# Experts in the order of their token counts, with places of 256 down to 32 tokens, in a mixture-of-experts kernel

## The reference

```python
def _moe(h, l, w_router, b_router, w_e_gate, w_e_up, w_e_down, w_s_gate, w_s_up, w_s_down):
    t = h.reshape(-1, shp[-1])                          # 576 tokens in all, 1024 wide
    s = jax.nn.sigmoid((t @ w_router[l]).astype(jnp.float32))
    _, sel = lax.top_k(s + b_router[l].astype(jnp.float32), TOP_K)        # TOP_K = 8 of 64
    g = jnp.take_along_axis(s, sel, axis=-1)
    g = g / jnp.sum(g, axis=-1, keepdims=True) * ROUTED_SCALE
    gates = ...                                         # g at the chosen experts, 0 elsewhere
    out = (jax.nn.silu(t @ w_s_gate[l]) * (t @ w_s_up[l])) @ w_s_down[l]
    for es in groups_of_8_experts:                      # w_e_gate, w_e_up: 1024 x 128, w_e_down: 128 x 1024
        a = jnp.einsum('nd,edf->nef', t, w_e_gate[l, es])
        u = jnp.einsum('nd,edf->nef', t, w_e_up[l, es])
        hid = jax.nn.silu(a) * u * gates[:, es, None]
        out = out + jnp.einsum('nef,efd->nd', hid, w_e_down[l, es])
    return out.reshape(shp)
```

## Time and profile before

| | us |
|---|---|
| median of 3 runs | 1312.42 (1308.63 to 1316.77) |
| the profiled execution | 1310.58 |
| its span, first to last instruction | 1308.6 |
| PE busy in the span | 1184.5 |
| gate_up's products (L1815) and down's (L1836) | 308.7 and 161.6 |
| turn_x (L1799) | 88.7 |
| granted clock, mean over the span | 0.962 of full |

### The profile page before, as it was taken

One profiled execution on the slowest core, in us unless ns is written; L12 is line 12 of the kernel. 1 busy time (PEld: TensorE's weight loads), 2 busy tenths in 40 slices (PEclk: granted clock), 3 DMA queues, 4 the chain that ended last, 5 costly groups with the idle time before them and its releaser, 6 DMA issues.

```text
span 1308.6 us, 26951 instructions
## 1 busy us (share of the span) xinstructions
PE 1184.5 (91%) x10827; PEld 719.5 (55%) x10827; DVE 552.3 (42%) x1349; ACT 390.0 (30%) x953; POOL 384.7 (29%) x447
## 2 busy tenths in 40 slices
PE   4899998899989898899769999999999999999796
PEld 1698885766744555454435555555555555555342
DVE  5418880243255477245627532332332222222245
ACT  3333331333345477111312222222222222222211
POOL 2233333423310232001012443434433434434200
PEclk8799998999989899899979999999999999999999
DMA  9222226543270000301629978878778778787296
GB/s 368 86 81 83 84 83 213 186 169 117 75 274 1 1 1 1 154 33 57 253 79 367 390 277 315 308 275 334 289 282 322 284 296 320 274 330 234 70 418 227
DMA packets 61738, 262.05 MB, mean 200 GB/s; under 512 B 24190, under 2 KB 24270, under 8 KB 47662
## 3 DMA queue, kind: packets, MB, share of 16 engines
q1 hardware_dynamic: 27648, 180.68, 37.1%
q0 software_dynamic: 33968, 79.66, 16.9%
HBM read 297.81 MB, written 53.69 MB: 269 GB/s over the span
## 4 chain that ended last, share of the span: by engine, by line
PE 66%; DMA 17%; DVE 8%; issue 5%; ACT 3%; POOL 2%; SPq 0%; POOLq 0%; DVEq 0%; ACTq 0%
PE bank L1815 15%; PE bank L1836 9%; DMA x_got<-x_dram,idx_tok 8%; PE bank L1670 5%; PE bank L1383 4%; PE bank L1799 4%; PE bank L1385 4%; PE bank L1384 4%; DMA pairs<-pair_dram 4%; PE bank L1489 3%; DMA pair_dram<-out_rows,idx_pair 2%; PE bank L1565 2%; PE bank L1411 1%; PE bank L1609 1%; PE bank L1821 1%
## 5 line engine op out<-in xcount | busy, mean ns | idle before, releaser
L1815 PE MATMUL bank<-slot,xt 128*32 128x256 f32 x5376 | 308.7, 382 | 12.3 <-issue 8.8
L1815 PEld LDWEIGHTS bank<-slot,xt 128*32 128x32 f32 x5376 | 180.2, 111 | 162.8 <-issue 68.3
L1836 PE MATMUL bank<-slot,hid_t 128*32 128x512 f32 x1344 | 161.6, 598 | 0.7 <-ACT hid_t L1348 0.7
L1048 POOL DMA_INDIRECT pair_dram<-out_rows,idx_pair x84 | 86.2, 1026 | 231.0 <-DVE out_rows L2304 182.7
L1383 PE MATMUL bank<-h_hi,w_hi 128*128 128x288 f32 x480 | 146.3, 305 | 0.0
L1384 PE MATMUL bank<-h_lo,w_hi 128*128 128x288 f32 x480 | 142.7, 297 | 0.0
L1385 PE MATMUL bank<-h_hi,w_lo 128*128 128x288 f32 x480 | 142.5, 297 | 0.0
L2304 DVE COPY out_rows<-bank 128x512 f32<-128x512 f32 x84 | 58.1, 692 | 171.0 <-DMA pair_dram<-out_rows,idx_pair 101.0
L656 POOL TENSOR_TENSOR w_lo<-w_stage,w_hi 128x1024 fp32r<-128x1024 f32 x29 | 69.6, 2402 | 131.2 <-ACT w_hi L1097 131.1
L1031 POOL DMA_INDIRECT x_got<-x_dram,idx_tok x84 | 85.8, 1021 | 72.4 <-DVE idx_tok L2282 43.2
L1354 ACT COPY out_rows<-bank 128x512 f32<-128x512 f32 x84 | 49.3, 587 | 168.5 <-DMA pair_dram<-out_rows,idx_pair 114.5
(11 more groups left out here) (338 smaller groups left out, 1565.9 us busy)
## 6 DMA issues: line engine op xcount, KB each, us to landing
slot<-in_w_moe SPq DMA_DIRECT2D x65, 1536.0 KB, 9.5
w_stage<-in_w_ada SPq DMA_DIRECT2D x32, 512.0 KB, 4.7
pairs<-pair_dram SPq DMA_DIRECT2D x16, 1024.0 KB, 9.9
w_stage<-in_w_in SPq DMA_DIRECT2D x30, 512.0 KB, 3.6
resid<-in_w_ada SPq DMA_DIRECT2D x2, 2048.0 KB, 13.2
w_out_sb<-in_w_out SPq DMA_DIRECT2D x1, 4096.0 KB, 15.2
o_t<-in_x_t SPq DMA_DIRECT2D x4, 576.0 KB, 5.6
feat<-in_w_ada SPq DMA_DIRECT2D x1, 2048.0 KB, 18.4
```

The costliest lines, as they stand in the source:

```text
L1048: g.indirect_dma_start(pair_dram, bass.IndirectOffsetOnAxis(ap=idx_pair[:, j, c:c + 1], axis=0), out_rows[:, i % 2, :], None, bounds_check ...
L1815: ins = mm(bank[2 + i % 2][r, 0:2 * P], xt[:, i % 2, k, r], slot_of(load)[:, 2 * P * k:2 * P * (k + 1)], start=(k == 0), stop=(k == KD - 1 ...
L1836: ins = mm(bank[4 + 2 * (i % 2) + c][r, :], hid_t[:, i % 2, r], slot_of(load)[:, 2 * D + 512 * c:2 * D + 512 * c + 512], start=True, stop= ...
```

## The change

The experts are sorted by their token counts at run time, and each place has a size by rank. The 64 ranks in groups of eight have 8, 4, 3, 3, 2, 2, 1 and 1 units of now 32 tokens (`CAPACITY`), 256 tokens down to 32. There are again 48 further places, of 64 tokens (two units), for what goes beyond an expert's own place. That is 192 + 96 = 288 units and 72 steps of four. With the counts above, 7 of the 48 further places are in use (22 before), and further place o is the o-th that is needed.

The places stand in eight like blocks of nine steps. Block g holds one rank of each group (8k + g) and six further places (8k + g):

| step of the block | places, with their units |
|---|---|
| 0, 1 | group 0 (8) |
| 2 | group 7 (1), further 0 (2), group 1 (first of 4) |
| 3 | group 1 (3 more), further 1 (first of 2) |
| 4 | further 1 (second), group 6 (1), group 2 (first two of 3) |
| 5 | group 2 (third), further 2 (2), group 3 (first of 3) |
| 6 | group 3 (2 more), further 3 (2) |
| 7 | group 4 (2), further 4 (2) |
| 8 | group 5 (2), further 5 (2) |

The six slots are parted: the shared expert and the ranked places go round slots 0 to 3 in their order, loaded by SP; the further places go round slots 4 and 5, loaded by POOL. A ranked place's address is now known only at run time: SP reads a row number from `idx_w` into a register ahead of each load, after the wait for the slot. Loads of ranked places start once `idx_w` is there.

The lists are made by unit in place of by expert: PE multiplies a choice matrix with the experts' values for three tiles of 128, 128 and 32 units (`unit_products`), ACT and DVE copy them and drop what belongs to an earlier unit (`find_units`), and DVE sorts four rounds (`PART // 8`) per tile: the first tile ahead of the loop, the second in steps 1 to 4, the third in steps 5 to 8, one round in a step. PE turns the second and third tile's lists at steps 6 and 11. Counting, ranking and the row numbers are worked out ahead of the loop, with PE's shared products cut into pieces between them. The gates' arithmetic leaves `choose` and goes into steps 12 to 16 as `find_gates`. POOL fills 52 small tables in place of 11 before it waits for the output projection.

The core of the diff:

```diff
-UNIT, PART = 96, 32
-N_OVER = (N_PROMPT + N_SAMPLE) * TOP_K // (UNIT + 1) + 1
+PART = 32
+CAPACITY = (8, 4, 3, 3, 2, 2, 1, 1)
+BEYOND, N_OVER = 2, 48
+BLOCK = (("rank", 0), ("rank", 7), ("over", 0), ("rank", 1), ("over", 1), ("rank", 6), ("rank", 2), ("over", 2),
+         ("rank", 3), ("over", 3), ("rank", 4), ("over", 4), ("rank", 5), ("over", 5))
...
-        def wait_slot_free(eng, load):
-
-            if load == 6:
+        def slot_of(i):
+            if PLACES[i][0] == "rank":
+                return slots[rank_places.index(i) % 4]
+            return slots[4 + over_places.index(i) % 2]
...
+        def wait_weights(eng, i):
+            if PLACES[i][0] == "rank":
+                n = rank_places.index(i)
+                eng.wait_ge(st_in[n % 4], 16 * (n // 4 + 1))
+            else:
+                n = over_places.index(i)
+                eng.wait_ge(ov_in[n % 2], 16 * (n // 2 + 1))
+
+        def wait_slot_free(eng, n, among):
+
+            ring = 4 if among is rank_places else 2
...
             else:
-                eng.wait_ge(d_full, 2 * (last_step_of(load - 6) + 1))
+                eng.wait_ge(d_full, 2 * (last_step_of(among[n - ring]) + 1))
...
+            sp.wait_ge(idx_w_ready, 1)
+            for n in range(1, N_EXPERTS + 1):
+                wait_slot_free(sp, n, rank_places)
+                u = PLACES[rank_places[n]][2]
+                row = nc.sync.value_load(idx_w[0:1, u:u + 1], min_val=P, max_val=N_EXPERTS * P)
+                sp.dma_start(slots[n % 4][:, :], io["w_moe"].rearrange("e p w -> (e p) w")[bass.ds(row, P), :])\
+                    .then_inc(st_in[n % 4], 16)
...
+            def load_over(n):
+                u = PLACES[over_places[n]][2]
+                wait_slot_free(pool, n, over_places)
+                g.indirect_dma_start(slots[4 + n % 2][:, :], None, io["w_moe"].rearrange("e p w -> (e p) w"),
+                                     bass.IndirectOffsetOnAxis(ap=idx_w[:, u:u + 1], axis=0),
...
             for i in range(1, N_STEPS + 1):
                 if i + 3 < N_STEPS:
                     gather(i + 3)
-                for load in range(6 + 1, N_UNITS + 1):
-                    if is_over(load) and last_step_of(load - 6) == i - 1:
-                        load_over(load)
+                for n in range(2, N_OVER):
+                    if last_step_of(over_places[n - 2]) == i - 1:
+                        load_over(n)
                 scatter(i - 1)
...
+            def unit_products(i):
+
+                a, n = LIST_TILES[i]
+                values, unit_places = unit_banks(i)
+                mm(values[0:n, :], chosen[:, a:a + n], value[:, 0:N_PROMPT], start=True, stop=True)
+                mm(bank[5][0:n, 0:N_SAMPLE], chosen[:, a:a + n], value[:, N_PROMPT:NT], start=True, stop=True)
+                mm(unit_places[0:n, :], chosen[:, a:a + n], place_t[:, 0:N_PROMPT], start=True, stop=True)
+                mm(bank[5][0:n, N_SAMPLE:2 * N_SAMPLE], chosen[:, a:a + n], place_t[:, N_PROMPT:NT], start=True, stop=True)\
+                    .then_inc(unit_full, 1)
...
+            def list_round(i, r):
+
+                n = LIST_TILES[i][1]
+                top, values = lists[0:n, i, 8 * r:8 * r + 8], unit_value[i][0:n, :]
                 chain(v.max(top, values))
-                if r + 1 < UNIT // 8:
-                    chain(v.match_replace(left, top, values, 0.0))
+                if r + 1 < PART // 8:
+                    chain(v.match_replace(values, top, values, 0.0))
...
+                for j in range(1, len(LIST_TILES)):
+                    if 0 <= i - SORT_AT[j] < PART // 8:
+                        list_round(j, i - SORT_AT[j])
+                if SHARED_AT <= i < SHARED_AT + 5:
+                    add_shared(i - SHARED_AT)
+                    find_gates(i - SHARED_AT)
```

More of the change, by code:

```diff
@@ L1 @@
 from contextlib import ExitStack
+import numpy as np
 import concourse.bass as bass
@@ L445, in build @@
-        idx_w = at("idx_w", [P, N_OVER], after("idx_tok"), U32)
+        key_col = at("key_col", [N_EXPERTS, 1], after("row_end"))
+        rank = at("rank", [N_EXPERTS, 1], after("key_col"))
+        own = at("own", [N_EXPERTS, 2], after("rank"))
+        left = at("left", [N_EXPERTS, 1], after("own"))
+        n_more = at("n_more", [N_EXPERTS, 1], after("left"))
+        begins = at("begins", [N_EXPERTS, 2], after("n_more"))
+        over_start = at("over_start", [N_EXPERTS, 1], after("begins"))
@@ new lines, in _ @@
+            for kind, k in BLOCK:
+                n = units_of(kind, k)
+                made(g.iota(by_block(unit_rank if kind == "rank" else unit_over, n), pattern=[[1, N_BLOCKS], [0, n]],
+                            base=N_BLOCKS * k, channel_multiplier=0, **iota))
+                step = 0 if kind == "rank" else PART * BEYOND
+                made(g.iota(by_block(unit_start, n), pattern=[[step, N_BLOCKS], [PART, n]], base=N_BLOCKS * step * k,
+                            channel_multiplier=0, **iota))
+                first += n
@@ L1708, in _, with turn_lists @@
+            def turn_lists(i, out):
+                a, n = LIST_TILES[i]
+                pe.wait_ge(listed, i + 1)
+                for b in range(4):
+                    ins = mm(out[PART * b:PART * b + PART, 0:n // 4], lists[0:n, i, :], ident[0:n, b:n:4], start=True,
+                             stop=True, skip_group_check=True)
+                ins.then_inc(lists_turned, 1)
             out_product(0)
@@ new lines, in _ @@
+            chain(v.scalar_tensor_tensor(out=scratch[:, :], in0=keys_, scalar=key_col[:, 0:1], in1=ones[:, :],
+                                         op0=ALU.is_gt, op1=ALU.mult, accum_out=rank[:, :]))
+            chain(v.scalar_tensor_tensor(out=scratch[:, 0:CAPACITY[0]], in0=rank_end[:, :], scalar=rank[:, 0:1],
+                                         in1=ones[:, 0:CAPACITY[0]], op0=ALU.is_gt, op1=ALU.mult, accum_out=own[:, 0:1]))
+            chain(v.tensor_tensor(left[:, :], key_col[:, :], expert_no[:, :], ALU.add))
@@ L2288, in x_half @@
+            find_units(0)
+            for r in range(PART // 8):
+                list_round(0, r)
+            find_units(1)
+            indices(0, bank[3][:, 96:96 + PART])
+            find_units(2)
+            shared_hidden()
+            rank_copies()
             def x_half(i):
```

520 lines of the change are left out of this document (256 added, 264 removed).

## The result

The changed kernel takes 1465.87 us at the median of 4 runs (1461.06 to 1468.73), beside 1311.81 of the kernel before (4 runs, 1308.63 to 1316.77): a ratio of 1.117, 95% interval 1.112 to 1.121. 1380 us were forecast, with a range from 1318 to 1425. The direction was right, the size was not: the change costs 154 us where +69 were forecast. The profiled execution took 1464.7 us, its span is 1463.0, its mean granted clock 0.903 (0.962 before).

A forecast was written before the change was run, and what follows sets the result against it. The prediction took TensorE to set the expert loop's pace, with DMA close behind. Its terms, -77 - 17 + 102 + 34 + 27 + 0 = +69 us, took 1310.6 to 1380 us, with a range from 1318 to 1425.

The forecast's parts named there:

- The named places: In each nine-step block, gate_ups 6, 7, 8 idle about 4 us for empty loads; 4 and 5 about 1.7 us.
- the term of the steps: Expert loop: 72 steps for 84, at 6.44 us each, -77 us.
- the old waits: Expert loop: of 27.6 us of waits before, 10 are kept, -17 us (between 0 and -27).
- terms 1 to 5: Expert loop: steps -77, old waits -17, further slots +102, clock +34, ranked slots +27 us.
- Term 6: Ahead of the expert loop: sorting idle time goes, unit products and small waits replace it, 0 us (-6 to +6).
- term 3: Further slots, steps 6 to 8 of each block: 24 waits of 4.2 us for empty loads, +102 us.
- Term 4: TensorE's clock after the 24 waits for further slots: 1.4 us more each, +34 us (0 to 68).
- Term 5: Ranked slots, steps 4 and 5 of each block: 16 waits of 1.7 us for direct loads, +27 us.
- The short round trips: Rival: empty loads land in 2.1 us, clock holds, old waits go altogether, 1289 us; chance 0.12.
- Everything at its upper end: Rival: empty loads at 4.7 us, clock 50 us, ranked loads at 9.4 us, 1478 us in all; chance 0.08.

The follow-up runs named there:

- the half loads: Changed kernel, with direct loads released together with an empty further load (steps 4, 5, 6 of a block) moving half their columns: 1407.35 us.
- The filling: Changed kernel, with 28 unused identity products on PE ahead of the weight waits of steps 6 to 8: 1440.09 us (48 products: 1496.42 us).
- the first experiment: Changed kernel, with SP issuing its direct load only after the count of the empty further load freed by the same down: 1347.73 us.
- the other order of places: Changed kernel, with only the order of the fourteen places in a block changed, rings of four and two slots kept: 1292.99 us.

## Why the prediction was wrong in size

**Where it was right.** The named places stalled, and but for 1.1 us no others; the term of the steps, the old waits and the signs of terms 1 to 5 hold. The clock fell as it said. Term 6 holds once it is measured from the first output product, which starts at 520.06 now and at 532.41 before, to gate_up(0):

```profile
520.06 1.19 PE L1720 MATMUL bank<-w_out_sb,o_t 128*128 128x512 f32 x1 [2.40 <-DVE o_t L2165]
```

```profile
532.41 1.19 PE L1670 MATMUL bank<-w_out_sb,o_t 128*128 128x512 f32 x1 [2.34 <-DVE o_t L2098]
```

655.65 - 520.06 = 135.6 us after, 666.49 - 532.41 = 134.1 before: +1.5, where 0 was forecast. The 12.4 us by which the output product starts sooner lie in code that the change does not touch; in the experiments' profiles, all alike up to there, it starts between 520.5 and 531.1. The one profile of the kernel before lies just above that range, so whether a part of the 12.4 is the change's stays open. The prediction's own test for the term (gate_up(0) between 660 and 673; it came at 655.65) was therefore a poor one: it held the wander of everything ahead.

**The step that failed is the landing in term 3.** "I take 3.2, nearest to those conditions." The rows at 3.2 and 4.7 were chosen because a direct load was in flight; how old it was I did not ask. In both, SP had issued it 7.2 us earlier, so most of it was through. Nor was it what the 4.7 waited for: that empty load landed at 756.64, the direct load at 754.82, and at 756.49 the gather that POOL had issued at 749.02:

```profile
x_got<-x_dram,idx_tok POOLq DMA_INDIRECT x1, 7.5
```

So an empty load can stand behind POOL's own gather as well as behind SP's load, whichever lands last. At the stall of 713.7 us in the changed kernel POOL had started nothing for 13 us, and only the direct load is left. After the change SP issues it 0.06 us ahead of the empty load, and the wait is all of it: 0.84 + 6.7 + 0.2 = 7.7 us for 4.2, which makes 184 for 102. The trace of before had the right row, unread. The direct load of 6.6 us at 1200.9 stands in the earlier trace rows; at 1201.6, 0.8 us behind it, POOL issued an empty load, and the DMA issues have it as

```profile
slot<-in_w_moe,idx_w POOLq DMA_INDIRECT x1, 6.0
```

which is 0.2 us behind the direct one again, in the kernel before. The prediction had used the one row for a price of ranked slots, and left out the other, which bears on its largest term.

The Trainium skill, page "DMA: Bandwidth & Descriptors", section "Queues, rings and completion order", has the rule: a DMA engine's increment of a semaphore lands only after every earlier write of that engine, across its queues. The order in the traces agrees: landings of 6.9, 4.4 and 2.1 us behind a whole, a half and no direct load. I weighed the Trainium skill's fixed cost of 2.0 us instead, which is what the quiet row shows (2.1) and not what a loaded queue does. The rule speaks of the increments alone, and the packets in the traces show more. Here are the DMA queues (packets, MB, share of the 16 engines) from 713.7 to 718.2 and from 718.2 to 720.7 us, and, in the run where SP waits, from 947.5 to 948.1, for the load issued at 946.0:

```profile
q1 hardware_dynamic: 89, 1.09, 74.9%
...
q0 software_dynamic: 329, 0.44, 47.9%
...
q0 software_dynamic: 144, 0.00, 10.5%
```

An empty load still has 144 small packets. With nothing ahead they start 1.6 us after the issue. Behind the direct load (q1) no packet of POOL's queue (q0) starts for 4.6 us. So the load's own packets are late, and not its count alone; what in the DMA engines holds them back, no run here shows.

**Term 4** was mis-sized, 1.4 us a gate_up for 2.3: the one row it used, gate_up(0) at 5.00, ran at a granted clock of 0.72, and the one shown above, of 6.04 us, at 0.60 (3.64 / 0.60 is 6.07). On the mean the lower level takes more of the gate_up the longer the stall: 1.3 us over 3.64 behind the 3.5 us of the run where SP waits, 2.0 behind the 5.5 of the half loads, 2.3 behind the 7.7 here. A single stall does not tell it: the longest gate_up of all, 6.51 us, followed one of 3.05. The filling brought the 56 us of steps 6 to 8 down to 8.

**Term 5** was a little high, 27 for 19: the stalls of step 4 came at 1.8, as forecast (1.7), those of step 5 at 0.5. The prediction priced the two alike, but a stall of step 4 gives the load for step 5 its time: where step 4 stood 2.2 us or more, step 5 did not stand at all. For step 4 the pieces were right too: SP's delay behind down was put at 0.9 and is 0.78, 0.56 of it the register read, and the landing was put at 7.0 and is 7.05 on the mean. The Trainium skill, page "DMA: Bandwidth & Descriptors", section "Latency and other measured facts", has a floor of about 600 ns for a `tensor_load`, which is the read's name in the trace. The trace does not bear the floor out: the read itself takes 270 ns at the median (below, nanoseconds at least, at the median and at most), and the rest of the 0.56 us is work on the register that follows it.

```profile
L856 SPq TENSOR_LOAD <-idx_w x64: 262/270/572, 623.5 to 1348.1; - x64
```

(Two small products in the prediction's term are off by one: 16 x 1.4 is 22 and 16 x 0.4 is 6.)

**The rivals.** The short round trips (1289) fell, yet their conditions came about where SP issued nothing: 3.05 us in the last two steps. "Everything at its upper end" (1478) came nearest in number, but by a split that is not the measured one (138 + 50 + 66 for 184 + 59 + 19). The range was closed above by a row, 4.7, that was no bound: a bound from the rows had to be a direct load's whole landing, 7.0 us or more, and 24 x (0.84 + 7.0 + 0.2) = 193.

## What to carry to other kernels

In these runs a DMA that moves nothing is not free, and it does not cost a fixed time: where a wait hangs on its count, price it at the landing of whichever load lands last among those in flight at its issue, on any queue, and count a load that goes out 0.2 us behind it with them. To get it through first, let the large load wait for its count, as SP did in the first experiment; the large one then starts later. So when a ring of buffers is parted or reordered, list for each place which step frees its slot, which step wants it, and what else the same step releases; a place with no whole step between stalled TensorE here, even an empty one. And when a price is taken from a row of the trace, take one in which the neighbours stand at the same distance in time, not only one in which they are present.

## What the runs showed of the hardware

- An empty indirect load of POOL lands 2.1 us after its issue on quiet queues, 4.4 behind a direct load of 768 KB issued 0.06 us ahead, 6.9 behind one of 1536 KB: each time 0.1 to 0.3 us behind the direct load, where both landings are on record. Where a gather of POOL was the last to land, in the kernel before and with the other order of places, it came 0.2 us behind the gather.
- SP's read of a row number from SBUF into a register takes 0.27 us, and with the work on the register 0.56 us between a wait and the issue that follows; read ahead of the wait, the load goes out 0.22 us behind down in place of 0.78.
- Idle time of one length is not one clock: in the kernel where SP waits, two gaps of 3.03 us in neighbouring steps were followed by gate_ups of 3.66 and 5.01 us. Work in the gap, 6.5 us of products that nobody reads, left the gate_up behind it at 3.66 us in 20 of 23 steps.
